# Where the modulation's rounds stand among the chunks of the input projection

## The reference

```python
def _layer(x, cond, pl, lambda_init, rope=None, ctx_kv=None):
    ada = (jax.nn.silu(cond) @ pl['w_ada'] + pl['b_ada']).astype(x.dtype)
    sh1, sc1, g1, sh2, sc2, g2 = jnp.split(ada[:, None, :], 6, axis=-1)
    h = x * (1 + sc1) + sh1
    y, k, v = _token_mixers(h, pl, lambda_init, rope, ctx_kv)
    x = _layer_norm(DEEPNORM_ALPHA * x + g1 * y, pl['ln1_g'], pl['ln1_b'])
    h = x * (1 + sc2) + sh2
    m = jnp.square(jax.nn.relu(h @ pl['w_mlp1'])) @ pl['w_mlp2']
    x = _layer_norm(DEEPNORM_ALPHA * x + g2 * m, pl['ln2_g'], pl['ln2_b'])
    return x, k, v
```

## Time and profile before

| | |
|---|---|
| median of 3 runs | 3781.52 us (3779.92 to 3782.53) |
| profiled execution | 3773.5 us, its span 3771.7 us |
| mean granted TensorE clock | 0.966 of full |
| TensorE busy (matmuls) | 3464.9 us, 92% |
| VectorE, ScalarE, GpSimd busy | 1928.8, 1101.1, 1334.9 us |
| first layer's chunks | about 70 to 414 us, value tiles to 471 us |
| second layer's chunks | about 1951 to 2230 us |

### The profile page before, as it was taken

How to read it: one execution, slowest core, us unless ns; L and a number is a source line. 1 busy time by engine, 2 the same in 40 slices (tenths; PEclk the granted TensorE clock), 3 DMA queues, 4 the chain that set the end, 5 groups by cost and what they waited for, 6 DMA issues and landing times. The chain is left out here.

```text
span 3771.7 us, 48305 instructions
## 1 busy us (share of the span) xinstructions
PE 3464.9 (92%) x18386; PEld 2904.5 (77%) x18386; DVE 1928.8 (51%) x2787; ACT 1101.1 (29%) x2020; POOL 1334.9 (35%) x682
## 2 busy tenths in 40 slices
PE   6899997898899999999988999788899999999996
PEld 3676876777788888888867777677777888888885
DVE  3047565875744434434552765387674344344347
ACT  3212154772511111111152113467534111111114
POOL 2336554101533232332364574430125323223232
PEclk8999998999999999999999999899999999999998
DMA  7577647512111111111117764744201111111101
GB/s 254 211 248 223 200 129 201 121 61 81 34 35 46 34 40 40 35 45 34 34 53 257 225 194 159 197 107 121 82 12 45 41 38 39 40 34 44 35 23 56
DMA packets 285272, 368.48 MB, mean 98 GB/s; under 512 B 16888, under 2 KB 203494, under 8 KB 283783
## 3 DMA queue, kind: packets, MB, share of 16 engines
q1 hardware_dynamic: 211586, 212.63, 19.5%
q10 hardware_dynamic: 73476, 152.83, 11.9%
HBM read 275.48 MB, written 81.53 MB: 95 GB/s over the span
## 5 line engine op out<-in xcount | busy, mean ns | idle before, releaser
L768 POOL TENSOR_TENSOR RH<-RAW,ONE 128x1024 fp32r<-128x1024 f32 x200 | 389.0, 1945 | 1534.2 <-PE PS L927 685.3
L927 PE MATMUL PS<-HH,RH 128*128 128x512 f32 (+1 forms) x2744 | 615.6, 368 | 69.7 <-issue 26.3
L772 POOL TENSOR_TENSOR RL<-RAW,RH 128x1024 fp32r<-128x1024 f32 x240 | 579.5, 2416 | 128.0 <-ACT RH L1903 107.0
L927 PEld LDWEIGHTS PS<-HH,RH 128*128 128x128 f32 x2744 | 471.6, 195 | 189.5 <-issue 96.7
L927 PE MATMUL PS<-HL,RH 128*128 128x512 f32 (+1 forms) x2744 | 584.6, 356 | 0.0
L927 PE MATMUL PS<-HH,RL 128*128 128x512 f32 (+1 forms) x2744 | 578.8, 353 | 0.0
L2553 DVE SCALAR_TENSOR_TENSOR XT<-PS,ADA,XT 128x512 f32<-128x512 f32 (+1 forms) x704 | 453.8, 662 | 244.1 <-PE PS L1419 240.6
L927 PEld LDWEIGHTS PS<-HL,RH 128*128 128x128 f32 x2744 | 466.1, 191 | 74.4
L927 PEld LDWEIGHTS PS<-HH,RL 128*128 128x128 f32 x2744 | 460.6, 189 | 70.9
L2078 ACT ACTIVATE RB<-PS 128x512 f32<-128x512 f32 (+1 forms) x192 | 101.1, 526 | 1391.0 <-PE PS L927 1391.0
L2537 DVE TENSOR_TENSOR PS<-PS,RB 128x512 f32<-128x512 f32 (+1 forms) x192 | 117.2, 610 | 746.4 <-ACT RB L2078 746.4
(11 more groups left out here) (264 smaller groups left out, 4505.6 us busy)
## 6 DMA issues: line engine op xcount, KB each, us to landing
RAW<-in_w_mlp_dram SPq DMA_DIRECT2D x128, 512.0 KB, 3.9
ADW<-in_w_ada_dram ACTq DMA_DIRECT2D x80, 512.0 KB, 5.5
RAW<-const_dram SPq DMA_DIRECT2D x52, 512.0 KB, 4.1
RAW<-in_w_in_dram SPq DMA_DIRECT2D x44, 512.0 KB, 4.7
z_scratch<-ZST ACTq DMA_DIRECT2D x40, 256.0 KB, 3.3
x_scratch<-XT SPq DMA_DIRECT2D x4, 2560.0 KB, 12.7
QH<-q_hi SPq DMA_DIRECT2D x32, 320.0 KB, 9.9
QL<-q_lo SPq DMA_DIRECT2D x32, 320.0 KB, 11.0
```

The costliest lines, as they stand in the source:

```text
L768: nc.gpsimd.tensor_tensor(RH[:, s, :], RAW[:, p, :], ONE[:].broadcast_to([128, 1024]), ALU.mult)\
L772: nc.gpsimd.tensor_tensor(RL[:, s, :], RAW[:, p, :], RH[:, s, :].bitcast(F32), ALU.subtract)\
L927: mm = pe.matmul(out, w[:, s, k * 128:(k + 1) * 128], m(k), start=(n == 0 and k == 0), stop=(n == 2 and k == KT - 1))
```

## The change

`ada_round_at` reads a table that `spread` works out: the rounds are laid at even distances over the columns of the chunks from a first chunk to the last but one, with at least one chunk between the second round of a block and the next block's first. In the first layer the first round stays after chunk 3; in the second it moves from 19 to 15. The load of round 0 is issued two iterations ahead of its round, where it was one.

| layer | rounds after chunks |
|---|---|
| first, before | 3, 5, 7 and every second chunk to 49 |
| first, now | 3 5 7 9 11 13 17 19 21 23 25 27 30 31 34 36 38 40 42 44 46 48 51 52 |
| second, before | 19, 21, 23 and every second chunk to 49 |
| second, now | 15 19 21 24 26 28 31 33 36 38 40 43 45 48 50 52 |

Turns stand at 6, 10, 14, 20, 24, 28, 32, 37, 41, 45, 49 and 53 now (before 6, 10, 14, 18 and every fourth chunk to 50), in the second layer at 20, 25, 29, 34, 39, 44, 49 and 53 (before 22, 26 and so on to 50).

```diff
--- before.py
+++ after.py
@@ -1,3 +1,4 @@
+import itertools
 import math
 from contextlib import ExitStack
 
@@ -124,9 +125,26 @@
     return max(x for x in range(at - 6, at) if down_bank(x) == down_bank(at)) + 1
 
 
+def spread(l):
+
+
+    first, n = (3, 2 * len(ADA_BLOCKS[0])) if l == 0 else (Z_FIRST - 3, 2 * len(ADA_BLOCKS[1]))
+    width = [CHUNKS[q][1] for _, q in Z_ORDER]
+    done = list(itertools.accumulate(width))
+    last = len(width) - 2
+    step = (done[last] - done[first]) / (n - 1)
+    at = [min(k for k in range(first, last + 1) if done[k] >= done[first] + step * r - 1) for r in range(n)]
+    for r in range(n - 2, -1, -1):
+        at[r] = min(at[r], at[r + 1] - 1 - r % 2)
+    return at
+
+
+ADA_AT = [spread(l) for l in range(DEPTH)]
+
+
 def ada_round_at(l, r):
 
-    return (3 if l == 0 else Z_FIRST + 1) + 2 * r
+    return ADA_AT[l][r]
 
 
 def ada_turn_at(l, b):
@@ -1772,7 +1790,7 @@
                     first_tiles(at)
                     if at == Z_FIRST - 1:
                         act.wait_ge(h_ready.sem, h_ready.at(l, 0))
-                    if at == ada_round_at(l, 0) - 1:
+                    if at == ada_round_at(l, 0) - 2:
                         load_ada(0)
                     modulation(at)
                     if q == 0 and i > 1:
```

## The result

| | before | changed |
|---|---|---|
| median of 12 runs | 3779.49 us (3758.79 to 3782.53) | 3786.34 us (3776.25 to 3799.3) |
| ratio of the timed pairs | | 1.0024, interval 1.0013 to 1.0036 |
| span of the profiled execution | 3771.7 us | 3787.3 us |
| first layer, chunk 2 to `UF` | 377.6 us | 385.8 us |
| second layer, first matmul to `UF` | 338.0 us | 340.9 us |

The account below looks back on a forecast made before the run. TensorE works nearly all the span, its ADW waits mostly following ScalarE's and VectorE's chains; +5.5 us in the first layer and +1.5 in the second make +7 on a median of 3781.52: 3788.5 us, 8 in 10 within 3774 to 3799.

Parts of the forecast that it names:

- What bounds it: Both projections: TensorE's ADW and AROW waits, 44.2 us, mostly follow chains through ScalarE and VectorE that TensorE doesn't pace.
- (a): First layer, load of round 0 an iteration sooner: first wait can go, chunks 4 and 5 then wait longer for GpSimd; 0.
- (b): First layer, chunks 14 to 29: round and turn move later, so the whole VectorE chain begins 2.5 us sooner.
- (c): First layer, neighbours 30 and 31: at least 2 us of wait, about 5 behind conv_store; net about 0 to -3.
- (d): First layer's end, neighbours 51 and 52: late load delays the value tiles, +5.5 us, between +1 and +9.
- (e): Second layer's start: early loads meet the spill; HYIN's issue 4 us later, VectorE's first unit +1, bounds -2 and +5.
- (f): Second layer, chunks 18 to 33: chain 1 us later, no gain at 33; +1, and +1 more for the lower clock.
- (g): Second layer, chunks 33 to 53: turn at 44 waits for the AROW copy; +1.5 for the layer, between -3 and +8.
- What would show it: Changed kernel: ADW waits 15 to 30 us per layer, AROW above 4.8, HYIN unit at 2025 to 2033, transposes near 427.
- even rounds give the waits back: Rival, both layers: evacuations late because TensorE stalls, so waits go; 3757, likelier 3769; chance 0.13.
- The neighbours cost little: Rival: neighbouring rounds cost +2, second layer's chain comes sooner, -3; about 3780.5 us; chance 0.20.
- The spill eats the early load: Rival, second layer: z stores land 5 to 8 us later and the layer follows; about 3795 us; chance 0.17.

Follow-up runs that it names:

- e11: Kernel before with rounds at every second chunk, but at even chunks from 20 on in both layers, first loads one iteration ahead; ratio 1.0011.
- e6: Kernel before with the third convolution of every Hyena unit replaced by a VectorE copy (output not the reference's); ratio 0.9962.
- e7: Changed kernel with the third convolution of every Hyena unit replaced by a VectorE copy (output not the reference's); ratio 0.9957.
- e1: Kernel before with only the first layer's load of round 0 issued an iteration sooner; ratio 0.9996.
- e10: Changed kernel with only the first layer's round at 51 moved to 50, the neighbours 30 and 31 kept; ratio 1.0001.
- e4: Changed kernel with two first-layer rounds moved, 30 to 29 and 51 to 50, so no two are neighbours; ratio 0.9999.
- e5: Changed kernel with the second layer's first round moved from 15 to 12, so both first loads go out before the spill; ratio 1.0008.
- e12: Table placed by ScalarE's iterations, even chunks between 24 and 52, second layer's round 0 at 12, against the kernel before; ratio 1.0004.
- e9: Changed kernel with the edits of e4 and e5 together; ratio 0.9982, 3771.56 us against 3777.44 of the kernel before.
- e0: Kernel before with its same rounds written as a list and nothing else changed; ratio 0.9995.
- e3: Kernel before with only the second layer's new table and earlier first load; ratio 1.0008.
- e2: Kernel before with only the first layer's new table and earlier first load; ratio 1.0021.

## Why the prediction was right

It said 3788.5 us, and 3786.34 was measured. The sum was +7: +5.5 in the first layer, +1.5 in the second. Over several profiles the stages are +7.1 and +2.8; the timed pairs give about +9. The paths named, VectorE's chain and the last pair, are the ones that the runs show. That the number came so near is in part luck: TensorE's lower clock behind its waits was taken too small in both layers, and in the second a wait behind the first value tile, which the sum left out, swallowed 4.1 of 7.0 us.

- **What bounds it.** Shown for the first layer, where e11 emptied the waits for ADW and e6 left the order alone; the first did nothing and the second took 8 us off. In the second, e6 and e7 bring the first value tile 4.2 and 10.5 us forward. None of the orders tried had any of the 44.2 us by the profile.
- **(a), 0.** Right as to the end, wrong on the way: chunk 5 comes 1.6 us late (35.33 in e1 and 35.42 in the changed kernel), which is regained by the first value tile (321.4 us behind chunk 2 in e1, 321.05 before).
- **(b), the chain 2.5 us sooner.** Not so: VectorE's first Hyena unit starts 116.0 us after chunk 2, where it was 116.5. The 1.6 us by which (a) delays chunk 5 took most of it: e1, which has the early load alone, starts the unit after 117.8, so the places of the rounds gave 1.8.
- **(c), at least 2 us at 31, net 0 to -3.** The wait is there, 3.44 us (1.36 in e10), and nets to nothing (e10 beside e4: 378.0 and 377.0).
- **(d), +5.5, from +1 to +9.** The mechanism is shown by e10. The size was under by 2.7 us in the profile and 1.6 in the mean. Term by term, with the 1.5 us by which chunk 2 is late taken off: the evacuation of 51 came 0.8 us sooner and not 2.5, the load took 8.0 us and not 8.7, and the round ran 0.6 us later than said (416.9 for 416.3). The lower clock cost 2.6 us where 1 was taken, which is the larger part. The rest is in the sum itself: it has the old transposes at 421.8, the row says 421.62, and 427.6 less that is 6.0 and not 5.5.
- **(e), HYIN's issue 4 us later, the unit 1 later, about 3.5 of wait at 15.** 3.9 and 1.0, and the wait 1.37. Over the profiles the unit is 2.2 late, between the 1 that was taken and the bound of +5. e5 gives it back.
- **(f), +1 to 2 at 33.** +4.3: 2136.14 - 18.0 = 2118.1, where it was 2113.88. Round 7 waits 7.54. Over the four kernels of each table it is +2.7 (163.5 and 166.2 us behind the layer's first matmul).
- **(g), +1.5.** This step was mis-sized most. The turn at 44 waits 6.69 us and comes at 2184.7 in the old time, 2 us later than foreseen, but turn and chunk 45 behind it take 9.6 us at the lower clock, and the round is at 2194.6, where about 2190 was said. The first value tile starts 7.0 us late. That the layer ends +2.9 at `UF` is due to the wait and the slow tile of the order of before (2.32 us and 1.4), which no step of (g) counted.
- **What would show it.** The transposes after the first value tile come at 431.37 (429.9 without the 1.5 by which chunk 2 is late), and 427 was said. HYIN's first unit starts at 2028.4 in the old time, within 2025 to 2033. AROW's wait rose to 12.1. ADW kept 14.2 and 11.3 us, where 15 to 30 was said: the new kind of wait, which no step named, holds the rest (2.1 and 4.6).

Of the rivals, "even rounds give the waits back" fell with the changed kernel and again with e11 and e12. "The neighbours cost little" holds for 30 and 31 and fell for 51 and 52, where the load issued at 410.46 took 8.0 us to its round. The estimate of 4.4 us by the Trainium skill (DMA: Bandwidth & Descriptors, Anatomy of one DMA — SWDGE (gpsimd) path) was too short there; it fits the loads of e5, which landed in 4.7 us. The section gives its times for a DMA issued by GpSimd, and these are issued by ScalarE. "The spill eats the early load" has the right sign; the load itself took 17.2 us to land, and VectorE's unit is 2.2 us late, about a third of the 5 to 8.

Not settled: what makes e9 faster by its timing, and whether "everything else" hides a part of a kernel's difference, since one profile each can't tell it from the drift of 15 us.

## What to carry to other kernels

Where a wait names a DMA, ask who issues it and what that engine was behind: here the load was late because ScalarE stood behind VectorE's unit, and every other placing of the rounds moved the same microseconds to another line of the chain of waits. A transfer that is started only when its buffer is read needs its own length in work between the two readers; laying things evenly by columns doesn't see that, and one such pair at the end of a stage, with nothing behind it that could absorb it, cost most of what the change cost. Count for a wait of TensorE also the matmuls behind it: 6.07 us of idle brought 2.6 us more at the lower clock. To see whether a stage is bound by a chain, shorten the chain and not the wait.

## What the runs showed of the hardware

**Idle time around one round.** Before, TensorE waits 1.95 us, does a round of 1.06, waits 0.89 and goes on at full clock. With the load sooner these become one idle of about 3 us, and the same matmuls run slower. Windows of the 5.4 us from chunk 4 on, first the kernel before, then the changed one (busy us of PE, PEld, DVE, ACT, POOL; granted clock, DMA share, GB/s):

```profile
111.03:116.50 5.47, 5.47 (x24) 4.43 (x24) 0.00 (x0) 1.59 (x3) 2.84 (x4) 1.00 0.74 221
```

```profile
112.65:118.00 5.35, 5.35 (x16) 4.25 (x17) 0.00 (x0) 1.58 (x3) 2.81 (x4) 0.68 0.76 236
```

0.68 of 2.4 GHz is a mean of stretches at 1.2 and at 2.4 (e1 has 0.69). The wait that was saved came back as matmuls at the lower clock: 1.6 us. Ten kernels agree: chunk 5 starts 33.6 to 33.8 us behind chunk 2 in the five with the late load (before, e0, e3, e6, e12) and 35.3 to 35.4 in the five with the early one (changed, e1, e2, e5, e7). But it is no rule for two short idles against a long one. In e11, with the late load, both are shorter than before, and chunk 4 runs at the lower clock all the same:

```profile
104.93 1.07 PE L981 MATMUL PS<-ADW,CONDS 128*32 128x512 f32 x8 [1.50 <-DMA ADW<-in_w_ada_dram]
106.62 3.60 PE L932 MATMUL PS<-HH,RH 128*128 128x512 f32 x8 [0.63 <-POOL RL L777]
```

In e11, as in e4, e9 and e10, chunk 5 starts after 34.5 to 34.8 us whichever way the load stands. These are the four whose chunk 2 begins sooner, and ahead of it their clock had risen earlier (the mean from 70 to 88 us is 0.90 to 0.97, and 0.72 to 0.81 in the ten others). The length of one idle doesn't settle it either: behind 3.44 us the round of 270.46 took 1.06 before, and in the changed kernel the one of 285.19, behind 3.44 us too, took 1.93.

**A copy that waits for GpSimd.** The copy in e6 and e7 takes 0.43 us for 128x512 where GpSimd is idle, and up to 2.37 where it works. VectorE's copy in e6, and GpSimd's operation beside it:

```profile
2050.21 2.37 DVE L2312 COPY CACC<-HYIN 128x512 f32<-128x512 f32 x1
```

```profile
2049.93 2.37 POOL L777 TENSOR_TENSOR RL<-RAW,RH 128x1024 fp32r<-128x1024 f32 x1
```

The copy ends 0.28 us behind GpSimd's; the one of 251.04, 1.70 us long, does the same behind a split that ends at 252.46, and so do the four others in e6 that overlap an operation of GpSimd (0.27 to 0.29 us). The convolution's own operations on the same tiles take 0.75 to 0.82 us in every unit. The Trainium skill (SBUF — State Buffer, SBUF: two separate sides) has it that a VectorE operation in its two-port mode and GpSimd take the shared ports from each other for a whole instruction; the trace agrees. It is why e6 shortened the second layer's units by 5.9 us and not by 9, as in e7.

**ADW's 1 MB.** In e5, where both loads go out before the spill, the halves land 4.7 us after issue (median of 4). In the changed kernel the first load, at 2011.23, lands after 4.9 us too; the second, at 2018.32, goes out beside SyncE's spill of 5 MB (2018.27) and lands after 17.2 (median of its two halves).
